# Product-key experts on one core: passes of 32 tokens with all heads instead of 128 tokens with two heads

## The chip, the core and the metric

The kernel runs on one core of a Trainium2 chip. Its engines work side by side: TensorE (PE, with its weight loads PEld), VectorE (DVE), ScalarE (ACT), GpSimd (POOL) and SyncE (SP), and 16 DMA engines move data. The metric is device time in microseconds, and less is better. A time is a median over runs.

## The reference

One step of a decoder layer for 512 new tokens of one sequence and 4 tokens of each of 8 running sequences, so 544 tokens of 1024 channels, all float32. After two recurrent branches comes the part that the change touches, an expert mixer with product keys:

```python
q = (tb @ w_q).reshape(blk, PEER_HEADS, 2, PEER_HALF)            # 8 heads, two halves of 128
s = jnp.einsum('thsk,hsnk->thsn', q, sub_keys)                   # 128 keys per half
sv, si = lax.top_k(s, PEER_TOPK)                                 # the best 16 of each half
cand = sv[:, :, 0, :, None] + sv[:, :, 1, None, :]               # 256 pairs
fv, fi = lax.top_k(cand.reshape(...), PEER_TOPK)                 # the best 16 pairs are the experts
g = jax.nn.softmax(fv, axis=-1)
act = jax.nn.gelu(jnp.einsum('thkd,td->thk', u_emb[idx], tb))
return jnp.einsum('thk,thkd->td', g * act, v_emb[idx])
```

There are 16384 experts, each a row u of 1024 numbers (its dot product with the token gives the activation) and a row v of 1024 numbers (added to the output with weight g times gelu). Each token uses 8 heads times 16 experts. The output is added to the residual and passes a last RMSNorm.

## The kernel before

The program is written engine by engine, and each engine's instructions run in the order of the code. Semaphores join the engines. The tables u and v lie side by side in HBM, so that one row of 8 KB holds both.

**Queries and scores.** 16 units of the weight stream give 16 query blocks (one head and half each) of 128 channels by 544 tokens. TensorE computes a unit (48 matmuls at L404), ScalarE copies it to `qs`, and one unit later TensorE multiplies it with the keys: four products of 128 tokens (L752) and one of the 32 sample tokens (L754). ScalarE copies the scores to `SC`. VectorE picks experts for the first pass while the later units run.

**Expert passes.** There are 17 passes. A pass takes 128 (token, head) partitions by 32 slots. In passes 0 to 15 the partitions are the 128 tokens of a tile, and the 32 slots are two heads of 16 experts; four passes make a tile complete. In pass 16 the 32 sample tokens stand four times on the partitions, each copy with two of the eight heads. Per slot:

- GpSimd gathers 128 rows of 8 KB by indirect DMA (L1331) into one of eight ring buffers. `gathers` waits until the slot that used the buffer before has been read by TensorE (`slot_free`, counted slot by slot).
- VectorE multiplies u with the token's channels and sums (L1768, called a dot below).
- After every two slots (GROUP = 2) five small VectorE instructions and a tanh on ScalarE (L1134) make the weights (L1772 to L1777).
- ScalarE writes each slot's weight on a diagonal 128x128 matrix (L1141), and TensorE multiplies it with v: two products of 128x128 by 512 columns (L788), summed in PSUM over all 32 slots of the pass. Each float32 product shows as two matmul records.

At the end of a pass `flush` (L1786) adds the sum to the residual; TensorE's next pass waits for that. `iteration` first copies the tile's channels to `tb` (L1796). The choice of experts for coming passes (`route_keys`, `route_pairs`, `route_rows`) is cut into pieces and stands between the groups. Passes 1 to 15 are one hardware loop on each of the four engines; passes 0 and 16 are straight code.

After pass 16 a product with `sel` (L799) adds the four copies of the sample tokens, and the last norms and stores follow.

## Time and profile before

| | us |
|---|---|
| time, median of 3 runs (2709.21 to 2720.2) | 2710.64 |
| time of the profiled execution | 2708.6 |
| its span, first to last instruction | 2706.6 |
| expert passes in it, first dot to last flush, 17 passes | 1518.8 |
| mean granted TensorE clock over the span | 0.908 |

All rows quoted below are of that one execution. The page gives shares of the whole span; the expert passes are the last 56% of it and have their own limits, so they are read by stretches. A granted clock of 1.00 is 2.4 GHz and 0.50 is 1.2 GHz.

### The profile page before, as it was taken

To read this page: it belongs to the slowest core of one execution; us is meant where nothing else is said; L and a number is where in the kernel's file an instruction comes from. 1 tells how busy PE (TensorE), PEld (TensorE's weight loads), DVE (VectorE), ACT (ScalarE), POOL (GpSimd) and SP (SyncE) were. 2 spreads that over 40 slices of the span, in tenths; PEclk is the share of its full clock that TensorE was granted. 3 is DMA by queue.
4 is the path that set the end of the run, shared out by engine and by line. 5 is a ranking of instruction groups with operands and counts; after the bars stand their busy time and mean duration, and the time that the engine had idled before them with its cause. 6 is when DMAs were issued, how large, how long until landed. Compare 5 with 4: busy or idle time off the path is not lost.

```text
span 2706.6 us, 34195 instructions
## 1 busy us (share of the span) xinstructions
PE 2130.6 (79%) x9927; PEld 1409.1 (52%) x9927; DVE 1767.8 (65%) x4439; ACT 657.1 (24%) x1597; POOL 1091.2 (40%) x822
## 2 busy tenths in 40 slices
PE   6988899999988898986777677766776676668776
PEld 6987778889977898952222223222322222223222
DVE  5887721143288434158787778777877787778785
ACT  4334300132255224321111111111111111111112
POOL 2553224365433342344444344434443443344342
PEclk9999967799998999999989898989989998898898
DMA  3220023222311232279999999999999999899997
GB/s 140 80 77 1 1 79 139 102 77 86 109 63 47 75 113 71 85 296 391 407 363 362 363 412 360 371 371 396 362 364 372 401 373 359 355 400 360 374 381 287
DMA packets 101508, 664.75 MB, mean 246 GB/s; under 512 B 11744, under 2 KB 12000, under 8 KB 29056
## 3 DMA queue, kind: packets, MB, share of 16 engines
q0 software_dynamic: 78336, 570.46, 52.7%
q1 hardware_dynamic: 20160, 71.92, 7.9%
q10 hardware_dynamic: 2880, 20.97, 2.0%
q8 instruction: 38, 0.62, 0.1%
q14 instruction: 94, 0.77, 0.1%
HBM read 650.38 MB, written 12.14 MB: 245 GB/s over the span
## 4 chain that ended last, share of the span: by engine, by line
DVE 33%; PE 25%; issue 24%; DMA 10%; POOL 4%; ACT 3%; DVEq 1%; POOLq 0%; SPq 0%; ACTq 0%
PE ps L404 12%; DMA s_r<-in_uv,s_gidx 9%; DVE s_r L1768 7%; PE ps L788 5%; DVE s_r L1380 4%; POOL s_r_rounded L1178 3%; DVE s_h L1768 2%; PE ps L641 2%; ACT s_gth L1134 1%; DVE s_r L1712 1%; PE ps L653 1%; DVE s_g L1773 1%; DVE s_g L1776 1%; DVE s_g L1772 1%; DVE s_g L1774 1%
## 5 line engine op out<-in xcount | busy, mean ns | idle before, releaser
L788 PE MATMUL ps<-s_r 128*128 128x512 f32 x1632 | 789.4, 632 | 236.5 <-ACT s_r L1141 235.6
L404 PE MATMUL ps<-s_r_rounded 128*128 128x272 f32 x5760 | 766.9, 296 | 35.7 <-POOL s_r_rounded L1178 10.6
L404 PEld LDWEIGHTS ps<-s_r_rounded 128*128 128x128 f32 x5760 | 753.4, 195 | 46.5 <-issue 28.2
L1331 POOL DMA_INDIRECT s_r<-in_uv,s_gidx x408 | 488.9, 1198 | 531.3 <-PE ps L788 441.5
L788 PEld LDWEIGHTS ps<-s_r 128*128 128x128 f32 x1632 | 309.6, 199 | 709.5 <-ACT s_r L1141 388.0
L1768 DVE CUSTOM_DVE_ANT_0 s_r<-s_r 128x1024 f32<-128x1024 f32 x408 | 486.9, 1222 | 59.6 <-DMA s_r<-in_uv,s_gidx 56.6
L1178 POOL TENSOR_TENSOR s_r_rounded<-s_r,s_r_rounded 128x1024 fp32r<-128x1024 f32 x120 | 305.5, 2547 | 469.6 <-ACT s_r_rounded L815 469.6
L788 PE MATMUL ps<-s_h,s_r 128*128 128x512 f32 x544 | 298.0, 698 | 208.6 <-ACT s_r L1141 208.6
L788 PEld LDWEIGHTS ps<-s_h,s_r 128*128 128x128 f32 x544 | 115.7, 224 | 385.9 <-ACT s_r L1141 252.2
L1134 ACT ACTIVATE s_gth<-s_g 128x2 f32<-128x2 f32 x272 | 55.4, 204 | 1036.8 <-DVE s_g L1774 1036.8
L1331 POOL DMA_INDIRECT s_h<-in_uv,s_gidx x136 | 156.1, 1148 | 344.5 <-PE ps L788 320.5
L815 ACT ACTIVATE s_r_rounded<-s_r 128x1024 fp32r<-128x1024 f32 x120 | 126.5, 1055 | 437.4 <-PE ps L404 437.2
L1141 ACT ACTIVATE s_r<-s_con,s_slot_w 128x128 f32<-128x128 f32 x544 | 188.7, 394 | 135.7 <-DVE s_slot_w L1777 134.2
L1768 DVE CUSTOM_DVE_ANT_0 s_h<-s_h,s_r 128x1024 f32<-128x1024 f32 x136 | 161.5, 1224 | 7.8 <-DVE s_tk_i L1716 5.1
L1380 DVE SCALAR_TENSOR_TENSOR s_r<-s_r,s_par 128x600 f32<-128x600 f32 x96 | 141.3, 1471 | 12.0 <-DVE s_r L1380 0.8
L1543 DVE TENSOR_TENSOR s_h<-ps,s_h 128x2048 f32<-128x2048 f32 x8 | 18.3, 2291 | 134.4 <-PE ps L653 134.4
L1776 DVE SCALAR_TENSOR_TENSOR s_g<-s_gth,s_act_z 128x2 f32<-128x2 f32 x272 | 43.8, 161 | 73.5 <-ACT s_gth L1134 73.5
L1796 DVE COPY s_r<-s_r 128x1024 f32 (+1 forms) x17 | 13.1, 768 | 79.6 <-issue 79.4
L1231 POOL TENSOR_TENSOR s_r<-s_r,s_ed 128x2048 f32<-128x2048 f32 (+1 forms) x5 | 19.3, 3860 | 112.3 <-DVE s_r L1462 83.7
L641 PEld LDWEIGHTS ps<-s_c_s,s_h 128*128 128x128 f32 x256 | 51.3, 311 | 8.8 <-issue 8.8
L1569 DVE TENSOR_TENSOR s_r<-s_r 128x544 f32<-128x544 f32 x16 | 11.9, 744 | 66.4 <-ACT s_r L977 66.4
L1594 DVE SCALAR_TENSOR_TENSOR s_r<-s_r,ps 128x544 f32 x8 | 5.8, 721 | 75.6 <-PE ps L404 75.6
(242 smaller groups left out, 1932.2 us busy)
## 6 DMA issues: line engine op xcount, KB each, us to landing
s_r<-in_wstream SPq DMA_DIRECT2D x120, 512.0 KB, 3.3
s_h<-in_sample_h_in ACTq DMA_DIRECT2D x8, 1024.0 KB, 5.0
out_sample_h_out<-s_h ACTq DMA_DIRECT2D x8, 1024.0 KB, 3.9
s_r<-in_uv,s_gidx POOLq DMA_INDIRECT x408, 10.2
s_r<-in_x SPq DMA_DIRECT2D x4, 544.0 KB, 6.8
s_r<-in_x SPq DMA_DIRECT2D x1, 2176.0 KB, 8.4
s_h<-in_uv,s_gidx POOLq DMA_INDIRECT x136, 9.0
out_y_prompt<-s_r SPq DMA_DIRECT2D x4, 512.0 KB, 9.9
```

The source lines that it names most:

```text
L404: last = pe.matmul(ps[:, 2 * p + h, 0:HALF], fr(wp[:, k, :]), fr(xp[:, k, h * HALF:(h + 1) * HALF]), start=start and k == 0 and t == 0, st ...
L641: last = pe.matmul(inter_out[:, k, b, :], h0[:, j, k * P:(k + 1) * P], c_s[:, k // 4, :].rearrange("p (b l) -> p b l", l=DEC_L)[:, b, :], ...
L653: last = pe.matmul(ps[:, 4 + g, :], bm[0:n, j, g * NST:(g + 1) * NST], xs2[0:n, g * 512:(g + 1) * 512], start=True, stop=True)
L788: last = pe.matmul(ps[:, h, :], diag[:, s % 4, :], ring[s % RING][:, D_MODEL + 512 * h:D_MODEL + 512 * (h + 1)], start=s == 0, stop=s == S ...
L815: act.activation(fr(whi[:, slot % 2]), wring[:, slot], ACT.Copy).then_inc(w_hi, 1)
L1134: act.activation(gth[:], g3[:], ACT.Tanh, scale=GELU_S).then_inc(gl_th, 1)
L1141: act.activation(diag[:, sl % 4, :], ident, ACT.Copy, scale=slot_w[:, j, q * GROUP + s:q * GROUP + s + 1]).then_inc(diag_ready, 1)
L1178: pool.tensor_tensor(fr(wring[:, slot]), wring[:, slot], fr(whi[:, slot % 2]), ALU.subtract).then_inc(w_lo, 1)
L1331: pool.indirect_dma_start(ring[sl % RING], None, a["uv"], bass.IndirectOffsetOnAxis(ap=gidx[:, j, s:s + 1], axis=0)).then_inc(gath[sl % RI ...
L1380: ch.link(dve.scalar_tensor_tensor(out=o, in0=row[:, k:k + CONVN], scalar=pcol(weights, blk, k), in1=o, op0=ALU.mult, op1=ALU.add))
L1768: ch.step(dve.tensor_tensor_reduce(out=u, in0=u, in1=tb, scale=1.0, scalar=0.0, op0=ALU.mult, op1=ALU.add, accum_out=act_z[:, j, k:k + 1]))
L1776: ch.link(dve.scalar_tensor_tensor(out=g1[:], in0=gth[:], scalar=1.0, in1=z, op0=ALU.add, op1=ALU.mult))
```

## The change

Each of the 17 passes now takes 32 tokens with all eight heads. Partition 32q + t is token t with heads 2q and 2q + 1; the 32 slots are again two heads of 16 experts. The number of passes, slots and gathered bytes is the same. What differs:

- The score products write straight in that layout: for each of four key blocks, 17 groups by 4 strips, each 32 tokens by 128 keys. The order of the query weights is permuted on the way in. Scores of four query blocks are computed together and copied with one ScalarE instruction.
- The token rows are put on the partitions four times by four DMAs from SP per pass (`tbg`, two buffers), for every pass. The copy to `tb` on VectorE is gone.
- Gelu and weights are made for four slots at once (BATCH = 4). The weight operand is `sel` (128x32) times the slot weight, one ScalarE instruction for each slot.
- The four products of a batch go to four strips of 32 output partitions, each with its own slot's v: `ps[32c:32c+32]`. Ring buffers come free by the batch (`v_free`). The sums of passes alternate between two pairs of PSUM banks.
- ScalarE copies a pass's four strips out (`empty`), and TensorE adds them with `sel` (`total`) during the next pass. `flush` runs once for every tile of 128 tokens, a pass later, and the last norm of a tile follows it.
- All passes are straight code; there is no loop. Routing for pass g + 1 (both slot halves) stands in pass g.

On TensorE, from the last query units to the first pass, before (L404 query units, L752 and L754 scores, L788 expert values):

```order
L404 MATMUL ps<-s_r_rounded 128x272 x48
L747 REGISTER_ALU
L752 ISA
L752 MATMUL ps<-s_r 128x128 x4
L754 MATMUL ps<-s_r 32x128
L772 REGISTER_ALU
L772 COMPARE_AND_BRANCH
L752 MATMUL ps<-s_r 128x128 x4
L754 MATMUL ps<-s_r 32x128
L788 MATMUL ps<-s_h,s_r 128x512 x4
L788 MATMUL ps<-s_r 128x512 x12
```

The same place now (L415 query units, L766 scores, L805 values):

```order
L415 MATMUL ps<-s_r_rounded 128x272 x192
L766 MATMUL ps<-s_r 32x128 x68
L415 MATMUL ps<-s_r_rounded 128x272 x144
L766 MATMUL ps<-s_r 32x128 x68
L805 MATMUL ps<-s_h,s_r 32x512
L805 MATMUL ps<-s_r 32x512 x3
L805 MATMUL ps<-s_h,s_r 32x512
L805 MATMUL ps<-s_r 32x512 x11
```

Five score products per unit have become 68 for every four units, and the last 68 stand behind the last unit. A batch is eight products of 32 rows instead of eight of 128 for the same four slots.

On VectorE, the turn from one looped pass to the next before (L1768 dots, L1772 to L1777 weights, L1796 the copy to `tb`, L1786 flush, L1721 and L1709 the start of a routing piece):

```order
L1776 SCALAR_TENSOR_TENSOR s_g<-s_gth,s_act_z 128x2
L1777 TENSOR_TENSOR s_slot_w<-s_g,s_gw 128x2
L1839 UNCONDITIONAL_BRANCH
L1839 ISA
L1796 COPY s_r<-s_r 128x1024
L101 ISA
L1784 REGISTER_ALU
L1786 ISA
L1786 TENSOR_TENSOR s_r<-ps,s_r 128x1024
L1721 ISA
L1721 COPY s_r<-s_r 128x256
```

The same turn now (L1754 dots, L1763 to L1771 weights of four slots, L1708 to L1715 the first routing piece):

```order
L1767 SCALAR_TENSOR_TENSOR s_g<-s_gth,s_act_z 128x4
L1771 TENSOR_TENSOR s_slot_w<-s_g,s_gw 128x4
L1754 ISA s_h,s_act_z<-s_h 128x1024
L1754 ISA s_act_z 128x1
L1754 ISA s_r,s_act_z<-s_r,s_h 128x1024
L1754 ISA s_act_z 128x1
L1708 MAX s_tk_v<-s_r 128x8
L1710 MAX_INDEX s_tk_i<-s_tk_v,s_r 128x8
L1711 MATCH_REPLACE s_r<-s_tk_v,s_r 128x128
```

Between the last weights of one pass and the first dot of the next nothing is left.

The core of the diff:

```diff
+GT = 32
+GROUPS = NCH * 4 + 1
 RING = 8
-GROUP = 2
+BATCH = 4
...
+        tbg = h0[:, 0, :].rearrange("p (a b) -> p a b", b=D_MODEL)
+        ring = [h0[:, 1, :]] + [R1[:, i * ROW:(i + 1) * ROW] for i in range(4)] + [R3[:, i * ROW:(i + 1) * ROW] for i in range(3)]
...
+            for g in range(GROUPS):
+                if g >= 2:
+                    sp.wait_ge(dotted, (g - 1) * SLOTS)
+                t0 = GT * (g % 4)
+                for q in range(4):
+                    sp.dma_start(tbg[GT * q:GT * (q + 1), g % 2, :], H2T[t0:t0 + GT, g // 4, :]).then_inc(tb_full[g % 2], 16)
...
+            def scores(i):
+                pe.wait_ge(q_ready, 4 * (i + 1))
+                if i:
+                    pe.wait_ge(sc_ready, i)
+                for g in range(GROUPS):
+                    for q in range(4):
+                        hs = (2 * q + i // 2) * 2 + i % 2
...
+                        last = pe.matmul(out, qs[:, q, GT * g:GT * (g + 1)], keys[:, hs, :], start=True, stop=True)
...
+            def total(g):
+                pe.wait_ge(evac_done, g + 1)
...
+                    last = pe.matmul(ps[o:o + GT, 2 + h, :], cc("sel"), evac[:, h, :], start=True, stop=True)
...
+            def values(g):
+                bank = 4 * (g % 2)
...
+                for b in range(BATCHES):
+                    if g and b == 4:
+                        total(g - 1)
+                    pe.wait_ge(lhs_ready, (g * BATCHES + b + 1) * BATCH)
                     for h in range(2):
-                        last = pe.matmul(ps[:, h, :], diag[:, s % 4, :],
-                                         ring[s % RING][:, D_MODEL + 512 * h:D_MODEL + 512 * (h + 1)],
-                                         start=s == 0, stop=s == SLOTS - 1)
-                    last.then_inc(slot_free, 1)
+                        for c in range(BATCH):
+                            n = g * SLOTS + b * BATCH + c
+                            last = pe.matmul(ps[GT * c:GT * (c + 1), bank + h, :], lhs[:, b % 2, c, :],
+                                             ring[n % RING][:, D_MODEL + 512 * h:D_MODEL + 512 * (h + 1)],
+                                             start=b == 0, stop=b == BATCHES - 1)
+                    last.then_inc(v_free, 1)
...
+            def batch(g, b):
+                m = g * BATCHES + b
+                act.wait_ge(gl_in, m + 1)
+                act.activation(gth[:, 0:BATCH], g3[:, 0:BATCH], ACT.Tanh, scale=GELU_S).then_inc(gl_th, 1)
...
+                for c in range(BATCH):
+                    k = b * BATCH + c
+                    act.activation(lhs[:, b % 2, c, :], cc("sel"), ACT.Copy,
+                                   scale=slot_w[:, k:k + 1]).then_inc(lhs_ready, 1)
...
+            def gather(g, s):
+                n = g * SLOTS + s
+                if s % TOPK == 0:
+                    pool.wait_ge(idx_ready, 2 * g + s // TOPK + 1)
+                if n == 1:
+                    pool.wait_ge(unit_done, UNITS)
+                if n >= RING:
+                    pool.wait_ge(v_free, (n - RING) // BATCH + 1)
...
             dve.wait_ge(sc_ready, 2)
-            route(0, 0, 0)
+            route(0, 0)
             dve.wait_ge(sc_ready, 4)
-            route(0, 1, 1)
+            route(0, 1)
+            dve.wait_ge(sc_ready, 5)
+            for g in range(GROUPS):
+                dve.wait_ge(tb_full[g % 2], 64 * (g // 2 + 1))
+                for s in range(SLOTS):
+                    if g + 1 < GROUPS:
+                        for j in range(2):
+                            if s == 11 * j + 2:
+                                route_keys(g + 1, j, 0)
+                            if s == 11 * j + 5:
+                                route_keys(g + 1, j, 1)
+                            if s == 11 * j + 8:
+                                route_pairs()
+                            if s == 11 * j + 11:
+                                route_rows(g + 1, j)
+                    if g and g % 4 == 0 and s == 25:
+                        flush(g // 4 - 1)
+                    if g and g % 4 == 0 and s == 30:
+                        final_norm(g // 4 - 1)
+                    dot(g, s)
+                    if s % BATCH == BATCH - 1:
+                        slot_weights(g, s // BATCH)
```

`scores(i)` counts as done when ScalarE has copied it (`sc_ready`); the fourth copy comes after the last unit.

## Rows read from the trace of the kernel before

**Rows 1.** The page: DMA share in 40 slices and GpSimd's queue (q0): packets, MB, share.

```profile
DMA  3220023222311232279999999999999999899997
q0 software_dynamic: 78336, 570.46, 52.7%
```

**Rows 2.** Busy us by engine and stretch, clock, DMA share, GB/s.

```profile
1176.70:2695.50 1518.80, 1076.08 (x2176) 425.30 (x2176) 1188.82 (x3702) 264.28 (x891) 639.04 (x539) 0.90 0.94 376
1195.00:1219.00 24.00, 18.14 (x40) 7.18 (x40) 16.72 (x50) 4.28 (x14) 10.64 (x10) 1.00 1.01 421
1978.00:1984.00 6.00, 0.06 (x1) 0.06 (x1) 5.00 (x21) 0.71 (x3) 0.00 (x0) 0.53 1.02 422
1984.00:1989.00 5.00, 5.00 (x7) 2.16 (x8) 4.35 (x17) 0.48 (x3) 0.50 (x1) 0.54 0.32 133
```

**Rows 3.** Waits of the expert passes: us in total, times, longest.

```profile
POOL s_r L1331 <- PE ps L788: 441.5, 216, 14.6
DVE s_r L1796 <- issue: 79.4, 14, 6.0
```

**Rows 4.** Timeline of one pair of slots: start, us, engine, line, operation, idle before.

```profile
1202.77 1.23 DVE L1768 CUSTOM_DVE_ANT_0 s_r<-s_r 128x1024 f32<-128x1024 f32 x1 [1.25 <-DMA s_r<-in_uv,s_gidx]
1205.06 0.16 DVE L1777 TENSOR_TENSOR s_slot_w<-s_g,s_gw 128x2 f32<-128x2 f32 x1
1205.25 0.69 ACT L1141 ACTIVATE s_r<-s_con,s_slot_w 128x128 f32<-128x128 f32 x2 [0.42 <-DVE s_slot_w L1777]
1205.71 3.70 PE L788 MATMUL ps<-s_r 128*128 128x512 f32 x8 [1.28 <-ACT s_r L1141]
1208.47 1.31 POOL L1331 DMA_INDIRECT s_r<-in_uv,s_gidx  x1 [2.32 <-PE ps L788]
```

**Rows 5.** Gathers issued at 1901.47 and at 1904.90: count, us from issue to landing.

```profile
s_h<-in_uv,s_gidx POOLq DMA_INDIRECT x1, 5.5
s_r<-in_uv,s_gidx POOLq DMA_INDIRECT x1, 8.3
```

**Rows 6.** TensorE timeline: strips of 64 rows, full products, and weight loads at low clock.

```profile
213.10 1.09 PE L465 MATMUL ps<-s_con,s_DA 128*64 128x128 f32 x16
214.13 1.16 PE L532 MATMUL ps<-s_r 128*128 128x128 f32 x8
1985.81 0.33 PEld L788 LDWEIGHTS ps<-s_h,s_r 128*128 128x128 f32 x1 [0.52 <-issue]
1986.67 0.33 PEld L788 LDWEIGHTS ps<-s_h,s_r 128*128 128x128 f32 x1 [0.52 <-issue]
```

**Rows 7.** Groups of the page: xcount, busy and mean ns, idle before and its cause.

```profile
L1134 ACT ACTIVATE s_gth<-s_g 128x2 f32<-128x2 f32 x272 | 55.4, 204 | 1036.8 <-DVE s_g L1774 1036.8
```

**Rows 8.** VectorE timeline at a loop turn and, from 2598.40, at the turn in straight code.

```profile
1969.24 0.16 DVE L1777 TENSOR_TENSOR s_slot_w<-s_g,s_gw 128x2 f32<-128x2 f32 x1
1975.12 0.77 DVE L1796 COPY s_r<-s_r 128x1024 f32 x1 [5.73 <-issue]
...
2598.40 0.69 DVE L1796 COPY s_r<-s_r 128x1024 f32<-128x1024 f32 x1
2602.75 1.22 DVE L1786 TENSOR_TENSOR s_r<-ps,s_r 128x1024 f32<-128x1024 f32 x1 [3.66 <-PE ps L788]
```

**Rows 9.** Timeline of routing on VectorE: second key piece, pairs, and the end of the rows.

```profile
1080.77 0.29 DVE L1709 MAX8 s_tk_v<-s_r 128x8 f32<-128x128 f32 x1
1082.68 0.18 DVE L1726 CAST s_tk_if<-s_tk_i 128x32 f32<-128x32 uint32 x1
1088.67 0.17 DVE L1744 SCALAR_TENSOR_TENSOR s_gidx<-s_tk_sel 128x16 uint32<-128x16 f32 x1
```

**Rows 10.** Timeline of a query unit and its scores, and of the first dot.

```profile
1083.55 6.27 PE L404 MATMUL ps<-s_r_rounded 128*128 128x272 f32 x48
1089.66 1.05 PE L752 MATMUL ps<-s_r 128*128 x8
1176.69 1.23 DVE L1768 CUSTOM_DVE_ANT_0 s_h<-s_h,s_r 128x1024 f32<-128x1024 f32 x1
```

More of the change, by code:

```diff
@@ L743, in _ @@
             pe.wait_ge(ld_late, 32)
-            def scores(q, p, first=False):
-                pe.wait_ge(q_ready, q + 1)
-                if not first:
-                    pe.wait_ge(sc_ready, q - 1)
-                for i in range(NCH):
-                    pe.matmul(ps[:, 4 + p, i * CH:(i + 1) * CH], qs[:, p, i * CH:(i + 1) * CH], keys[:, q, :],
-                              start=True, stop=True)
-                pe.matmul(ps[0:DEC, 6 + p, 0:NKEYS], qs[:, p, SEQ:TOK], keys[:, q, :],
-                          start=True, stop=True).then_inc(sc_mm, 1)
@@ L757, in query @@
-            def query(i, j, first=False):
-                if not first:
-                    pe.wait_ge(q_ready, i * RINGW + (j - 1))
-                unit(i * RINGW + (U_WQ + j), j, j % 2, hn_parts, blocks=(hn_ready, KT) if first and j == 0 else None)
+            def scores(i):
[5 more added lines that the diff above has]
+                        hs = (2 * q + i // 2) * 2 + i % 2
+                        out = ps[GT * q:GT * (q + 1), 4 + g // 4, (g % 4) * NKEYS:(g % 4 + 1) * NKEYS] if g < GROUPS - 1 \
+                            else ps[GT * q:GT * (q + 1), i, 512 - NKEYS:512]
+                        last = pe.matmul(out, qs[:, q, GT * g:GT * (g + 1)], keys[:, hs, :], start=True, stop=True)
+                last.then_inc(sc_mm, 1)
@@ L793, in _ @@
-            experts(0)
-            with pe.Fori(1, ITERS) as it:
-                experts(it)
-            pe.wait_ge(flushed, ITERS)
-            for h in range(2):
-                last = pe.matmul(ps[0:DEC, 2 + h, :], cc("sel"), X2T[:, TILES - 1, 512 * h:512 * (h + 1)],
-                                 start=True, stop=True)
-            last.then_inc(fin_mm, 1)
+            for i in range(HS // RINGW):
+                for j in range(RINGW):
+                    n = i * RINGW + j
+                    if n >= 2:
+                        pe.wait_ge(q_ready, n - 1)
+                    unit(U_WQ + n, j, j % 2, hn_parts, blocks=(hn_ready, KT) if n == 0 else None)
+                    if i and j == 0:
+                        scores(i - 1)
@@ L1158, in _ @@
-            squares = SC[:, 0:2, :].rearrange("p a b -> p (a b)")
-            softmax_exp(1)
-            experts(0)
-            with act.Fori(1, ITERS - 1) as it:
-                experts(it)
-            experts(ITERS - 1, True)
-            act.wait_ge(flushed, ITERS + 1)
-            token_norms(NCH, TILES, TILES, squares)
+            for n in range(HS):
+                keep_query(n)
+                if n >= RINGW and n % RINGW == 1:
+                    keep_scores(n // RINGW - 1)
+                if n == 2 * RINGW + 3:
+                    softmax_exp(0)
@@ new lines, in _ @@
+            softmax_exp(1)
+            for g in range(GROUPS):
+                for b in range(BATCHES):
+                    if b == 2 and g + 1 < GROUPS:
+                        softmax_exp(2 * g + 2)
+                    if b == 3 and g:
+                        empty(g - 1)
+                    if b == 4 and g + 1 < GROUPS:
+                        softmax_exp(2 * g + 3)
+                    if b == 6 and g and g % 4 == 0:
+                        token_norm(g // 4 - 1)
+                    batch(g, b)
@@ L1747, in route_rows @@
+                dve.wait_ge(ex_ready, 2 * g + j + 1)
                 ch.link(dve.reciprocal(tk_r[:], tk_sum[:]))
[L1748 to L1778 removed]
@@ L1851, in _blocks @@
+            flush(NCH)
+            final_norm(NCH)
 def _blocks(w, kb):
```

334 lines of the change are left out of this document (124 added, 210 removed).

## The prediction

> **What bounds the kernel now.** I read the page first, then the expert passes by stretches, then the waits of GpSimd and VectorE, then one pair of slots in the timeline. The page shows that the DMA engines are nine tenths busy through the expert passes, and that GpSimd's queue, the gathers, carries 570 of the 665 MB moved [rows 1]. The passes take 1518.8 us, that is 89.3 for each of 17. In them the DMA share is 0.94 at 376 GB/s, while in the steady stretch it is 1.01 at 421 GB/s [rows 2]. A slot is 128 rows of 8 KB, 1,048,576 bytes; at 421 GB/s that is 2.49 us, so 32 slots need 79.7 us and 17 passes 1355. The DMA bounds the passes, and 164 us are lost beside it. They are lost at the turns: the stretch after one shows the DMA at 0.32 of its share [rows 2]. There GpSimd waits for TensorE to free a ring buffer, 14.6 us at the longest [rows 3], because VectorE stands still in front of L1796 for 5.7 us at each loop turn (79.4 us in 14 of them) [rows 3, 8], then flushes and routes before its first dot.
>
> So two questions decide: what becomes of the turns, and whether a ring of eight buffers that comes free four at a time still keeps the DMA supplied.
>
> **What goes.** The loop turn (5.7 us), the copy to `tb` (0.8) and 15 of the 17 flushes (1.2 each) leave VectorE, and 16 rounds of small weight instructions per pass become 8. A round takes 1.22 us from the dot's end to the weights' end [rows 4], so 9.8 us per pass go. Of the turn not all can be had: in straight code the stall is gone, but VectorE waits 3.66 us for TensorE's last product [rows 8]. The new code avoids that too, since the flush comes a pass later. VectorE's pass is then 32 dots at 1.15 (36.8), 8 rounds (9.8) and two routings of some 10.5 (below), 68 us. It no longer bounds anything; nor does TensorE. Were the ring long enough, a pass would be 79.7 plus the token rows (four DMAs of 128 KB, 0.5 MB at 421 GB/s, 1.25), that is 80.9 us: 142 us less in all. This is the most the change can bring to the passes.
>
> At the loop turn the Trainium skill bears on this (Runtime: NRT & Kernel Launch, Instruction fetch mechanics): a taken branch out of the instructions already fetched stops the engine until its target has come, so it advises to unroll. The trace agrees with 5.73 us.
>
> **What the batch adds.** The four buffers of batch b come free together and are gathered into for batch b + 2. The loop of one batch, from the landing of its fourth gather, by [rows 4] where nothing else is named:
>
> - dot 1.23, then the round 1.22, then 0.03 to ScalarE;
> - four weight operands of 128x32. The trace has 0.20 for 128x2 [rows 7] and 0.345 for 128x128 (half of 0.69). Bounds 0.8 and 1.4 for four; I take 0.24 each, 0.96, nearer the small one. Then 0.11 to TensorE, which waits for all four;
> - eight products, 16 records. Does it run four strips at once? Sixteen records of 64-row strips, alternating between two strips, take 1.09 us, where eight full records of as many columns take 1.16 [rows 6]: two strips run side by side. Four strips don't occur in the trace. Bounds: four at a time 4 record times, two at a time 8; I take 4, since the two strips show no loss at all. A record time is 0.86 us at a granted clock of 0.54 [rows 2, 6], half of that at full clock, where eight records take 3.70 [rows 4], so 0.3 stays as the tail of the last. TensorE would work under 4 us in every 10 and idle the rest. Idle from the last pass's end, it stood at 0.53 and came back at 0.54 [rows 2]. So I take the low clock: 4 x 0.86 + 0.3 = 3.7 (full clock 2.0);
> - from the products' end to the gather 0.76: the first slot's four records end at 1205.71 + 1.7 + 0.3 = 1207.71, and the gather starts at 1208.47;
> - issue to landing 5.5 where nothing is ahead [rows 5], and three more slots at 2.49, 7.47.
>
> Sum 21.0 us for a loop, in which two batches pass: 10.5 us per batch, 83.9 per pass. Supply alone would give 10.1. The ring is the bound, by little, and every microsecond in the loop counts half, eight times a pass.
>
> Two things lengthen it. Routing stands in front of single dots: the second key piece takes 1.9 us, pairs and rows together 6.2 [rows 9], and some 0.5 for the softmax scale; say 1.9, 1.9, 3.3 and 3.4. Where dots wait for landings, each leaves 2.49 - 1.15 = 1.3 us. Pieces before slots 11 and 19 (the last of a batch) delay it by 2.1 and 2.0, that before slot 22 by 0.8 at slot 23; the others fit. 4.9 us in one of two alternating chains are 2.5 per pass. And gathers into an emptied queue come slowly: issued at 1901.47 and landed 5.5 later, at 1906.97; the one issued at 1904.90 landed at 1913.2 [rows 5], with one more between. Two slots in 6.2 us instead of 5.0: 1.2 late per burst. Bounds 0 (the queue rarely empties) and 4.8 per pass (each burst pays); I take 4.0, since the ring-bound case empties it every time. Below 0 it can't be, as the DMA share is full already.
>
> A pass: 83.9 + 2.5 + 4.0 = 90.4 us, 1536.8 for 17, against 1518.8: **+18.0**. Bounds from these pieces alone (operands 0.8 to 1.4, restarts 0 to 4.8): 85.8 to 93, or -60 to +62.
>
> The rule that speaks against the change is in the Trainium skill (TensorE: Matmul & The Clock Gate, Why this matters for your kernels): idle gaps between bursts of matmuls bring the slow clock back. The trace agrees, with 0.53 after the turn. Of the strips the same page (Part 3: Packing small matmuls) says that outputs in different groups of 32 partitions run at the same time, and gives 2.38 times the speed for three; by that the batch takes somewhat more than my 4 record times, and the sum would move by some us per pass to the slow side. No row here shows three or four.
>
> **Start and end.** The first dot came at 1176.69 [rows 10], 5.1 us after the last unit. Now the last scores, their copy and the whole second routing stand behind that unit. 68 products are 136 records: at 0.068 per record with two strips [rows 6] 9.2 us, with four 4.6; I take 5. The copy of 2048 columns: between 128x2 and 128x128 an element costs 1.1 ns, 2.3 us. Query copy 0.6. Routing 1.9 + 8.1 + 0.5 = 10.5 [rows 9]. First dot 18.4 after the unit: +13.3. The eight buffers are full by then, and nothing can be gathered until the first batch is through, so the delay stays. The scores before the last unit: 15 times 1.3 us (1.05 and the sample's 0.3) [rows 10] against three times 5: -4.5. At the end, a batch instead of a pair before the last product, and a copy by ScalarE (its 128x1024 some 1.1): +3. Final norms of earlier tiles and the stores lie beside other work. SP's copies of token rows wait for dots of a pass before and are done long ahead; if not, the first dot of a pass would wait some 3 us.
>
> Sum: 2708.6 (the profiled execution) + 18.0 + 13.3 - 4.5 + 3 = 2738.4. The median of before is 2 us above the profiled execution, which I leave out. A measurement of this kernel can tell 0.5% (13.5 us) from no change.
>
> **Rivals.**
>
> 1. *The loop is short enough.* Full clock (2.0 us instead of 3.7), or operands at 0.2 and no slow restarts, make the supply the bound: 80.9 plus what routing still delays, some 2.5 to 4.5: 83.4 to 85.4 a pass. Taken 84.9: 17 x -4.4 = -75, with +12 for start and end 2646. For it: the DMA never starves in the steady stretch, where one slot at a time is freed [rows 2]. Against: the clock at 0.53.
> 2. *Strips run two at a time, or one after another.* 8 record times, partly at the higher clock as the burst is long: 5.6 to 7.2 us. Loop 22.9 to 24.5, per pass 92 to 98, plus 6.5: 98.5 to 104.5. +156 to +258, and +16: 2880 to 2980. That is the case in which the change doesn't do what it says. For it: every float32 product has two records for the same strip, which can't run together. Against: two strips show twice the rate.
> 3. *Straight code stalls.* VectorE's code grows to 17 passes. If each block of new code cost a stop like the 5.7 of a turn, ten of them would come on top: 2738 + 57 = 2795. Against: pass 16, straight behind the loop, starts without a stop [rows 8].
>
> **Chances.** Forecast 0.53, rival 1 0.25, rival 2 0.13, rival 3 0.09. The forecast's own range is 2690 to 2790. The range for the time takes rival 1 in and stops before most of rival 2: 2645 to 2860. Slower by over 0.5%: 0.66 of the forecast (35), rivals 2 and 3 (22): 0.57. Faster: nearly all of rival 1 and a tenth of the forecast: 0.29. Within: 0.14.
>
> **What would show it.** The turn: no idle of 5.7 on VectorE, and no wait for the flush. The loop: GpSimd's gathers in bursts of four, each burst 0.8 after the batch's last product, DMA share below 0.95 throughout instead of 1.01 with dips. TensorE: four records starting together, batches of 3.7 us, granted clock near 0.5. A pass of 90 us between first dots; the first dot 18 us after the last unit. I am wrong if the DMA share stays at 1.0 between batches (then rival 1), if a batch takes over 5 us on TensorE (rival 2), or if VectorE waits for "issue" inside passes (rival 3).

## The result: 2846 us, slower by 5%, and the profile after

| | before | after |
|---|---|---|
| median, us | 2709.9 (2709.1 to 2720.2, 4 runs) | 2846.3 (2845.0 to 2851.5, 4 runs) |
| ratio, with its 95% interval | | 1.050 (1.047 to 1.053) |
| profiled execution: span | 2706.6 | 2842.7 |
| first dot, last dot | 1176.69, 2688.82 | 1181.73, 2822.87 |
| a pass (mean of 12, first dot of pass 3 to first dot of pass 15, counted from 0) | 89.9 | 97.5 |

The direction was forecast (+30 us), the size was not (+136). The two spans split it: the first dot is 5.0 us later, first to last dot takes 1641.1 us instead of 1512.1 (+129.0), the end 2.0 more. So nearly all of it is in the passes. All means by pass or by batch below are over the same 12 passes, worked out from the start times of the dots and gathers in the timeline and from the landings. Batches 0 to 7 of a pass are its groups of four slots.

The page after: TensorE's granted clock, DMA share and queues, and VectorE's dots. Through the passes the DMA share of [rows 1] was mostly 9, and now about every third slice is an 8. Queue q1, which carries the copies of token rows, had a share of 7.9% and has 8.8%.

```profile
PEclk9999967999998999756556655666665556566555
DMA  3220033222211322589988998899989898998997
q0 software_dynamic: 78336, 570.46, 51.5%
q1 hardware_dynamic: 23040, 80.05, 8.8%
L1754 DVE CUSTOM_DVE_ANT_0 s_r<-s_r,s_h 128x1024 f32<-128x1024 f32 x476 | 580.0, 1224 | 406.6 <-DMA s_r<-in_uv,s_gidx 404.3
```

The passes by stretches, after (columns as in [rows 2]: stretch, length, busy us of five engines, clock, DMA share, GB/s): the whole, then an emptied queue and the time that follows it.

```profile
1300.00:2800.00 1500.00, 473.27 (x2044) 83.73 (x2036) 966.12 (x2701) 181.50 (x706) 529.08 (x494) 0.60 0.91 352
...
2022.00:2024.50 2.50, 1.31 (x8) 0.00 (x0) 2.36 (x8) 0.00 (x0) 0.38 (x1) 0.50 0.43 174
2024.50:2026.00 1.50, 0.00 (x0) 0.00 (x0) 0.98 (x2) 0.00 (x0) 1.20 (x2) 0.50 0.46 76
2026.00:2030.00 4.00, 0.00 (x0) 0.00 (x0) 2.47 (x8) 0.94 (x5) 2.17 (x3) 0.50 0.89 326
```

The dips of the loop turns are gone, but the share is 0.91 at 352 GB/s where [rows 2] has 0.94 at 376. The dips that took their place come four times a pass, one in front of each even burst: in the pass from 2046 to 2143 the share falls to 0.49, 0.35, 0.35 and 0.00 in stretches of 2 us. Behind one, a share of 0.89 moves only 326 GB/s, where the steady stretch of before moved 421 at 1.01. GpSimd waits for TensorE in front of each burst and no longer in front of single gathers, to answer [rows 3] (us in total, times, longest):

```profile
POOL s_h L1335 <- PE ps L805: 634.0, 67, 21.2
...
POOL s_r L1335 <- PE ps L805: 301.4, 67, 7.2
```

134 waits are one for each batch after the first two. Those in front of `s_h`, which holds slot 0 of the eight, belong to batches with an even number and are twice as long. "Even" and "odd" below are the numbers of batches; a burst is the four gathers that a freed batch lets start. One batch from its last dot to the next gather, in answer to [rows 4]:

```profile
2001.73 1.23 DVE L1754 CUSTOM_DVE_ANT_0 s_r<-s_r,s_h 128x1024 f32<-128x1024 f32 x1 [1.21 <-DMA s_r<-in_uv,s_gidx]
2004.03 0.16 DVE L1771 TENSOR_TENSOR s_slot_w<-s_g,s_gw 128x4 f32<-128x4 f32 x1
2004.29 0.96 ACT L1155 ACTIVATE s_r<-s_con,s_slot_w 128x32 f32<-128x32 f32 x4 [0.49 <-DVE s_slot_w L1771]
2005.30 3.51 PE L805 MATMUL ps<-s_r 128*32 128x512 f32 x16 [6.46 <-ACT s_r L1155]
2009.63 1.63 POOL L1335 DMA_INDIRECT s_r<-in_uv,s_gidx  x1 [4.58 <-PE ps L805]
```

From the dot's end (2002.96) to the gather are 6.67 us; my terms were 1.22 + 0.03 + 0.96 + 0.11 + 3.7 + 0.76 = 6.78. This half of the loop was right to 0.1 us. The other half was not. These are two even bursts: the gathers of the first (slots 24 to 27) start at 2024.12 and no routing stands in front of its dots; the second (slots 0 to 3 of the next pass) starts at 2046.69. Columns: start, us, engine, line, operation, idle before and what ended it.

```profile
2024.12 0.93 POOL L1335 DMA_INDIRECT s_h<-in_uv,s_gidx  x1 [9.12 <-PE ps L805]
2029.58 1.23 DVE L1754 CUSTOM_DVE_ANT_0 s_h<-s_h 128x1024 f32<-128x1024 f32 x1 [0.41 <-DMA s_h<-in_uv,s_gidx]
2033.78 1.23 DVE L1754 CUSTOM_DVE_ANT_0 s_r<-s_r,s_h 128x1024 f32<-128x1024 f32 x1 [1.83 <-DMA s_r<-in_uv,s_gidx]
2036.24 1.22 DVE L1754 CUSTOM_DVE_ANT_0 s_r<-s_r,s_h 128x1024 f32<-128x1024 f32 x1 [1.23 <-DMA s_r<-in_uv,s_gidx]
2038.69 1.22 DVE L1754 CUSTOM_DVE_ANT_0 s_r<-s_r,s_h 128x1024 f32<-128x1024 f32 x1 [1.22 <-DMA s_r<-in_uv,s_gidx]
...
2046.69 1.58 POOL L1335 DMA_INDIRECT s_h<-in_uv,s_gidx  x1 [7.15 <-PE ps L805]
2053.57 1.23 DVE L1754 CUSTOM_DVE_ANT_0 s_h<-s_h 128x1024 f32<-128x1024 f32 x1 [1.26 <-DMA s_h<-in_uv,s_gidx]
2057.39 1.22 DVE L1754 CUSTOM_DVE_ANT_0 s_r<-s_r,s_h 128x1024 f32<-128x1024 f32 x1 [2.59 <-DMA s_r<-in_uv,s_gidx]
2062.57 1.23 DVE L1754 CUSTOM_DVE_ANT_0 s_r<-s_r,s_h 128x1024 f32<-128x1024 f32 x1 [2.16 <-DMA s_r<-in_uv,s_gidx]
2066.09 1.23 DVE L1754 CUSTOM_DVE_ANT_0 s_r<-s_r,s_h 128x1024 f32<-128x1024 f32 x1 [2.29 <-DMA s_r<-in_uv,s_gidx]
...
2074.18 1.36 POOL L1335 DMA_INDIRECT s_h<-in_uv,s_gidx  x1 [11.03 <-PE ps L805]
```

My sum had the fourth slot landed 13.0 us after its burst's first gather (5.5 + 3 x 2.49). Here it is 14.6 in the first burst, where only the second slot is late (4.2 instead of 2.5 after the first), and 19.4 in the second, into which SyncE puts the four copies of token rows:

```profile
2051.10 2.90 SPq L395 DMA_DIRECT2D s_h<-s_r  x4
```

In the mean the loop of an even batch takes, from its first gather to the next one into the same buffer:

| batches | 0 to 2 | 2 to 4 | 4 to 6 | 6 to 0 | sum |
|---|---|---|---|---|---|
| forecast, bare | 21.0 | 21.0 | 21.0 | 21.0 | 84 (90.5 with its 6.5 for routing and restarts) |
| after | 26.7 | 24.1 | 24.2 | 22.4 | 97.4 |

Last, start and end, to answer [rows 10]: scores, their copy, and the last total.

```profile
1165.44 3.92 PE L766 MATMUL ps<-s_r 128*32 128x128 f32 x136 [0.71 <-ACT s_r L1110]
...
1169.43 1.88 ACT L1114 ACTIVATE s_r<-ps 128x2048 f32<-128x2048 f32 x1 [4.04 <-PE ps L766]
...
2831.23 3.55 PE L790 MATMUL ps<-s_r,s_con 128*32 128x512 f32 x4 [1.14 <-ACT s_r L1137]
```

### The profile page after: what moved, and what is told of

Same layout as the page of the kernel before. It is cut to its first block, busy times and chain, and to the rows that moved or that the text cites. A ratio compares the mean times of both kernels' runs of the same rounds, so it can differ in the third digit from the quotient of the medians.

```text
span 2842.7 us, 30578 instructions
## 1 busy us (share of the span) xinstructions
PE 1567.5 (55%) x10375; PEld 1072.1 (38%) x10375; DVE 1636.6 (58%) x3698; ACT 590.4 (21%) x1412; POOL 1030.9 (36%) x822
## 4 chain that ended last, share of the span: by engine, by line
issue 27%; DMA 25%; PE 23%; DVE 12%; POOL 9%; ACT 2%; DVEq 0%; POOLq 0%; SPq 0%; ACTq 0%
DMA s_r<-in_uv,s_gidx 24%; PE ps L415 12%; POOL s_r L1335 5%; PE ps L805 5%; DVE s_r L1381 3%; POOL s_r_rounded L1184 3%; DVE s_r L1754 2%; PE ps L652 2%; ACT s_r L1155 1%; PE ps L664 1%; POOL s_h L1335 1%; PE ps L506 1%; PE ps L766 1%; DVE s_r L1379 1%; DMA s_rgh<-in_rgh 1%
## 5 line engine op out<-in xcount | busy, mean ns | idle before, releaser
L1754 DVE CUSTOM_DVE_ANT_0 s_r<-s_r,s_h 128x1024 f32<-128x1024 f32 x476 | 580.0, 1224 | 406.6 <-DMA s_r<-in_uv,s_gidx 404.3
L415 PE MATMUL ps<-s_r_rounded 128*128 128x272 f32 x5760 | 764.0, 295 | 37.0 <-POOL s_r_rounded L1184 11.8
L415 PEld LDWEIGHTS ps<-s_r_rounded 128*128 128x128 f32 x5760 | 752.6, 195 | 45.9 <-issue 26.3
L805 PE MATMUL ps<-s_r 128*32 128x512 f32 x1904 | 484.8, 1043 | 418.2 <-ACT s_r L1155 418.2
L805 PE MATMUL ps<-s_h,s_r 128*32 128x512 f32 x272 | 240.6, 1040 | 724.7 <-ACT s_r L1155 724.7
L805 PEld LDWEIGHTS ps<-s_h,s_r 128*32 128x32 f32 x272 | 36.5, 159 | 913.4 <-ACT s_r L1155 591.1
L1335 POOL DMA_INDIRECT s_h<-in_uv,s_gidx x68 | 91.0, 1338 | 634.2 <-PE ps L805 634.0
L805 PEld LDWEIGHTS ps<-s_r 128*32 128x32 f32 x1904 | 79.4, 158 | 619.9 <-ACT s_r L1155 530.6
L1149 ACT ACTIVATE s_gth<-s_g 128x4 f32<-128x4 f32 x136 | 27.9, 205 | 1145.7 <-DVE s_g L1765 1145.7
L1155 ACT ACTIVATE s_r<-s_con,s_slot_w 128x32 f32<-128x32 f32 x544 | 130.1, 310 | 66.9 <-DVE s_slot_w L1771 66.9
L1754 DVE CUSTOM_DVE_ANT_0 s_h<-s_h 128x1024 f32<-128x1024 f32 x68 | 83.2, 1223 | 77.6 <-DMA s_h<-in_uv,s_gidx 77.1
L1708 DVE MAX8 s_tk_v<-s_r 128x8 f32<-128x128 f32 x68 | 19.6, 288 | 82.2 <-ACT s_r L1114 82.0
L652 PE MATMUL ps<-s_c_s,s_h 128*128 128x4 f32 x256 | 52.1, 340 | 1.1 <-ACT s_r L963 1.1
L1570 DVE TENSOR_TENSOR s_r<-s_r 128x544 f32<-128x544 f32 x16 | 11.9, 743 | 66.3 <-ACT s_r L989 66.3
```

Of the source, the lines that this page charges most:

```text
L415: last = pe.matmul(ps[:, 2 * p + h, 0:HALF], fr(wp[:, k, :]), fr(xp[:, k, h * HALF:(h + 1) * HALF]), start=start and k == 0 and t == 0, st ...
L652: last = pe.matmul(inter_out[:, k, b, :], h0[:, j, k * P:(k + 1) * P], c_s[:, k // 4, :].rearrange("p (b l) -> p b l", l=DEC_L)[:, b, :], ...
L805: last = pe.matmul(ps[GT * c:GT * (c + 1), bank + h, :], lhs[:, b % 2, c, :], ring[n % RING][:, D_MODEL + 512 * h:D_MODEL + 512 * (h + 1)] ...
L1155: act.activation(lhs[:, b % 2, c, :], cc("sel"), ACT.Copy, scale=slot_w[:, k:k + 1]).then_inc(lhs_ready, 1)
L1335: pool.indirect_dma_start(ring[n % RING], None, a["uv"], bass.IndirectOffsetOnAxis(ap=gidx[:, g % 2, s:s + 1], axis=0)).then_inc(gath[n % ...
L1754: dve.tensor_tensor_reduce(out=u, in0=u, in1=tbg[:, g % 2, :], scale=1.0, scalar=0.0, op0=ALU.mult, op1=ALU.add, accum_out=act_z[:, s:s + ...
```

## The experiments

All times are medians; the ratio is to the kernel before, measured beside each, with its interval. "A pass" is the mean defined above, of one profiled execution.

One thing beside the passes moves these times by some 10 us. The last 136 score records take 3.9 us in `after` and in eight other traces, and 12.7 to 14.3 us in those of `ring10`, `rows_once`, `routes_first`, `rows_once_routes`, `rowspe8` and `ring10_rowspe_routes`, where TensorE stops between them ("issue", 4 to 6 us in all) and its granted clock is 0.74 to 0.81 instead of 1.0. The first dot is late by as much. Why was not tested. So small differences are read from the column "a pass".

| run | us | ratio | a pass |
|---|---|---|---|
| after | 2846.3 | 1.050 (1.047 to 1.053) | 97.5 |
| ring10 | 2638.8 | 0.972 (0.968 to 0.976) | 84.9 |
| rows_once | 2806.2 | 1.034 (1.029 to 1.038) | 94.8 |
| routes_first | 2820.7 | 1.039 (1.034 to 1.044) | 95.7 |
| before_free4 | 2916.8 | 1.074 (1.069 to 1.080) | 101.8 |
| dose | 2929.9 | 1.079 (1.077 to 1.081) | 102.5 |
| warm | 2855.7 | 1.052 (1.050 to 1.054) | 98.2 |
| batch2 | 2664.0 | 0.981 (0.979 to 0.983) | 87.2 |
| batch2_ring10 | 2639.8 | 0.973 (0.971 to 0.974) | 85.6 |
| warm_even | 2832.9 | 1.043 (1.041 to 1.046) | 97.0 |
| half | 2732.2 | 1.007 (1.005 to 1.009) | 91.1 |
| ring9 | 2714.6 | 1.001 (0.999 to 1.003) | 89.2 |
| ring10_rowspe | 2578.0 | 0.950 (0.949 to 0.952) | 81.4 |
| rows_once_routes | 2777.0 | 1.024 (1.020 to 1.028) | 92.5 |
| rowspe8 | 2809.7 | 1.036 (1.034 to 1.039) | 94.8 |
| ring10_rowspe_routes | 2586.1 | 0.954 (0.952 to 0.957) | 81.6 |

### Is it the loop from landing to free buffers?

The loop theory: eight buffers, freed four at a time, don't cover landing, dots, weights and products, and what stands in that loop sets the pace. The rival: the DMA's own work (slower gathers, token rows) sets it.

**ring10**, two more buffers:

```diff
-RING = 8
+RING = 10
+            + [R2[:, XB * TOK + 2 * D_MODEL:XB * TOK + 2 * D_MODEL + ROW], R4[:, WORK - 4 * TOK:WORK - 4 * TOK + ROW]]
...
+                if n == RING - 1:
+                    pool.wait_ge(sc_mm, HS // RINGW)
```

> The changed kernel with ten ring buffers instead of eight (the two more lie where the query copies and old convolution channels were). If the loop of the buffers bounds it (theory: ten buffers make the loop of 10 slots, so a pass falls from 97.3 us towards the DMA's 81), the time falls by 8 to 14 us a pass, 140 to 230 in all, to 2620 to 2710. If it is the DMA that has become slower (the copies of token rows, 4 KB pieces between the gathers), more buffers change little: over 2800.

2638.8 us. Two buffers take 208 us away, though batch, strips, rounds and clock are the same. Its passes, columns as above:

```profile
1300.00:2590.00 1290.00, 470.38 (x2016) 83.55 (x2016) 950.71 (x2677) 180.05 (x700) 564.62 (x489) 0.62 1.01 404
```

The DMA share is 1.01 over the whole stretch; TensorE's clock, 0.62, is as low as in the slow kernel. So once the queue stays full, neither clock nor strips nor straight code cost anything that shows.

**ring9**, one more buffer:

```diff
-RING = 8
+RING = 9
+            + [R2[:, XB * TOK + 2 * D_MODEL:XB * TOK + 2 * D_MODEL + ROW]]
```

> The changed kernel with nine buffers: one gather of each burst is issued a batch earlier, so 2.5 us of transfer stand in the queue when the others are freed. Loop theory: the empty stretch between two bursts (1.1 us per batch by the DMA packets) and most of the slow first packets go; a pass of 85 to 89 us, 2640 to 2710, between eight buffers (97.5 us a pass) and ten (84.9). If slow restarts depend on the bursts and not on the emptied queue, it stays above 2750.

2714.6 us, a pass of 89.2, 5 us above the expected range and the same time as the kernel before. One buffer is worth 8.3 us a pass, the second 4.3, after which the supply is the bound.

**dose**, one unused full product in front of every batch:

```diff
+                    for _ in range(1):
+                        pe.matmul(ps[:, 6, :], ident, H2T[:, 0, 0:512], start=True, stop=True)
```

> The changed kernel with one more full product (512 columns, its result unused) on TensorE in front of every batch's products: some 1.7 us at the low clock, put into the loop from landing to free buffers. Loop theory (the eight buffers come free four at a time, and what stands in the loop counts half per batch): 1.7 x 4 loops x 17 passes = +116 us, 2940 to 2970. Supply theory (the DMA engines, with slow restarts and token rows, set the pace, and TensorE is beside the path): within 15 us of 2846. If the clock rises from the work that is added, the loop theory gives less, 2850 to 2900.

2929.9 us, +83.6, 10 us under the expected 2940. From last dot to gather it takes 1.6 us more (8.3), and a pass 5.0 more, where the loop theory says 4 x 1.6 = 6.4. The rest is given back while the landings wait.

**half**, 8 of 16 records per batch:

```diff
-                    for h in range(2):
+                    for h in range(1):
```

> The changed kernel without the products of the second 512 value columns (their part of the output is not computed): 8 records per batch instead of 16, 1.7 us less between the weights and the free buffers of every batch, nothing else. Loop theory: minus 6.8 us a pass at most, by the same slope as one product more gave (5.0 us a pass for 1.6 us): 2846 - 85 to - 116, 2730 to 2760. Supply theory: within 15 us of 2846.

2732.2 us, -114, as expected: the tail, from the end of a batch's last dot to the gather it sets free, is 5.09 instead of 6.72, and a pass 6.4 shorter (4 x 1.63 = 6.5). A microsecond in the loop counts four times a pass, as the prediction had it.

**before_free4**, the kernel before with its buffers freed in fours:

```diff
-                        pool.wait_ge(slot_free, it * SLOTS + (sl - RING + 1))
+                        pool.wait_ge(slot_free, it * SLOTS + ((sl - RING) // 4 * 4 + 4))
```

> The kernel before with one part of the change alone: GpSimd waits until the four slots of a batch have all been read before it gathers into the first of them; weights stay in pairs and products per slot. Loop theory: the last of four slots is read some 7 us after the first, so the supply starves oftener; +30 to +100 us, 2740 to 2810. Rival (freeing by four costs nothing, the loss lies in what precedes the products): within 15 us of 2710.

2916.8 us: +201, more than twice what I expected, and slower than the changed kernel. Coarse freeing alone costs the kernel before 11.9 us a pass, without any strips. It has the turns besides, and four of its slots occupy TensorE for two pairs of 3.7 us one after the other.

**batch2**, two slots per batch, two batches side by side in the four strips:

```diff
-BATCH = 4
+BATCH = 2
...
-                            last = pe.matmul(ps[GT * c:GT * (c + 1), bank + h, :], lhs[:, b % 2, c, :],
+                            d = 2 * (b % 2) + c
+                            last = pe.matmul(ps[GT * d:GT * (d + 1), bank + h, :], lhs[:, b % 2, c, :],
...
-                                             start=b == 0, stop=b == BATCHES - 1)
+                                             start=b < 2, stop=b >= BATCHES - 2)
```

> The changed kernel with batches of two slots instead of four: two batches share the four strips, buffers come free two at a time, and VectorE has 16 rounds of small instructions per pass as before the change. Loop theory: the loop of a batch is 5.5 + 2.5 + 1.2 + 6.3 = 15.5 us for eight buffers, under the 19.9 that the supply needs, so the DMA never empties: VectorE's work (80 us a pass) and the supply (81) bound it together, 83 to 87 a pass, 2610 to 2690. If instead the work in straight code, the token rows by SP or the products in strips cost the time, it stays above 2800.

2664.0 us with eight buffers. The same work, freed in twos, is 182 us faster and beats the kernel before by 1.9%: it is the batch of four that empties the queue. Here the DMA share is full:

```profile
1300.00:2620.00 1320.00, 713.21 (x2016) 123.46 (x2016) 1038.99 (x3281) 218.18 (x821) 538.64 (x488) 0.74 1.00 394
```

**batch2_ring10**, both:

> Batches of two slots and ten buffers. Loop theory: the loop is no limit with either, so nothing is added: within 15 us of the better of the two alone (2639 with ten buffers). With ten buffers and batches of four a pass takes 84.9 us of which 82.7 are the gathers' own packets; here VectorE has 9.8 us more of small instructions, and if that is what bounds it, it is slower than 2639 by 10 to 60 us.

2639.8, the same as ten buffers alone, but the start hides a difference: first to last dot takes 1438.2 us against 1427.2 in `ring10`, 0.7 us a pass more (85.6 against 84.9), and `ring10` has the late first dot. VectorE's eight additional rounds cost little, not nothing.

### Which of the two chains, and the clock

**warm**, six unused products behind every batch:

```diff
                     last.then_inc(v_free, 1)
+                    for _ in range(6):
+                        pe.matmul(ps[:, 6, :], ident, H2T[:, 0, 0:512], start=True, stop=True)
```

> The changed kernel with six full products (results unused) on TensorE behind every batch, after its buffers are set free, so that TensorE is not idle between batches. Loop theory: with the full clock the products of a batch take 2.0 instead of 3.7 us, the loop 22.7 instead of 24.4, a pass 90.7: 2730 (2715 to 2760). If the clock stays low, six products take 10 us, stand in front of the next batch at times and make it slower than 2846. Supply theory: 2846 whatever the clock.

2855.7, nothing gained, a miss. TensorE in the timeline of this run (L805 the products, L810 the unused ones):

```profile
2003.91 1.06 PE L805 MATMUL ps<-s_h,s_r 128*32 128x512 f32 x1 [6.98 <-ACT s_r L1157]
2004.77 1.06 PE L805 MATMUL ps<-s_h,s_r 128*32 128x512 f32 x1
2005.62 1.06 PE L805 MATMUL ps<-s_h,s_r 128*32 128x512 f32 x1
2006.48 1.06 PE L805 MATMUL ps<-s_h,s_r 128*32 128x512 f32 x1
2007.49 6.31 PE L810 MATMUL ps<-s_r,s_con 128*128 128x512 f32 x12
...
2013.73 1.92 PE L805 MATMUL ps<-s_r 128*32 128x512 f32 x16
2015.59 5.42 PE L810 MATMUL ps<-s_r,s_con 128*128 128x512 f32 x12
```

An even batch comes after 7 us of idle and runs at 1.2 GHz (a record every 0.86 us), the odd one right behind it at 2.4 GHz (16 records in 1.92). Odd tails fell to 5.6 us on average, even ones stayed at 6.75, and the loop at 24.6: the odd burst's first dot came 10.8 instead of 9.3 us after its gather, for it stands in the queue behind the even one. What the odd chain wins, it waits. That is against the prediction's "counts half": a gain in one of the two chains alone brought nothing.

**warm_even**, 12 behind odd and 3 behind even batches:

```diff
+                    for _ in range(12 if b % 2 else 3):
```

> The changed kernel with 12 unused full products behind every batch with an odd number and 3 behind every even one. With six behind each, the trace showed that only the odd batches ran at the full clock (5.1 to 5.7 us from the last dot to the next gather, the even ones 6.7 to 6.8 as before), and that the time did not move. Theory: the even batches are the ones whose gathers go into an empty queue; their loop alone sets the pace, and the odd ones wait behind them in the queue. Then the even loop 1.7 us shorter gives up to 6.8 us a pass, less where the odd chain takes over: 2750 to 2800. If both chains count alike, as my prediction had it, the six products would have brought 30 us already, and this brings about as much as that, nothing: 2840 to 2860. If twelve products last longer than the gap, the time is above 2860.

2832.9, 13 us less: below the 2840 to 2860 of equal chains, not the 2750 to 2800 either. Twelve products last 10.6 us and stand in front of the even batch at times, so its tail fell only to 6.44. That is inconclusive for the even chain alone; `half`, which shortens both, is the clean test.

### What lengthens the landings

**rows_once** leaves out 60 of the 68 copies of token rows (the output of passes 2 to 16 isn't computed from their own rows):

```diff
+                if g >= 2 and g % 4 != 2:
+                    continue
...
-                for q in range(4):
+                for q in range(4 if g < 2 else 0):
...
-                dve.wait_ge(tb_full[g % 2], 64 * (g // 2 + 1))
+                dve.wait_ge(tb_full[g % 2], 64)
```

> The changed kernel with the token rows copied for the first two passes only; later passes use those rows again, so 60 of the 68 copies of 128 KB are left out and the output is not the reference's. If the copies slow the gathers beyond their own 1.25 us a pass, the time falls by the missing 7 us a pass or more, below 2740. If the loop bounds it, at most their own share goes: 2820 to 2846.

2806.2, -40: below the 2820 of the one theory and far above the 2740 of the other. The loop from batch 0 to 2 fell from 26.7 to 23.2, that from 2 to 4 took 1.0 of it back.

**routes_first**, each routing piece in front of a batch's first dot:

```diff
-                            if s == 11 * j + 2:
+                            if s == 16 * j:
...
-                            if s == 11 * j + 5:
+                            if s == 16 * j + 4:
```

(and `+ 8`, `+ 12`; the second exponential moves from batch 4 to 6)

> The changed kernel with each piece of routing in front of the first dot of a batch (slots 0, 4, 8, 12, 16, 20, 24, 28) instead of slots 2, 5, 8, 11, 13, 16, 19, 22. By the loop theory a piece in front of the last dot of a batch lengthens the loop: my sum had 2.5 us a pass for it, 42 in all: 2800. If pieces anywhere make VectorE late by their sum, the time stays within 15 us of 2846.

2820.7, -26 and short of the expected 2800; some 10 us are lost to the late first dot. The loops 2 to 4 and 4 to 6 fall from 24.1 and 24.2 to 22.6 and 23.1; the loop 0 to 2 rises from 26.7 to 27.2.

**rows_once_routes**, both edits together:

> The changed kernel with both edits that were run alone: the token rows are copied only for the first two passes (output of the others is not computed from their own rows), and the routing pieces stand one in front of each batch's first dot. Alone they gave 40 and 26 us. If what is left over of the error is the slow restarts of the DMA queue, the two add up: 2780 (2770 to 2790), a pass of 93 to 94 us, still 3 to 4 above the 90.4 of my sum. If the two were the whole error, a pass comes to 90.4 or less, below 2735.

2777.0, as expected: a pass of 92.5, with even loops of 23.7, 22.7, 23.3 and 22.7 us, nearly alike. With rows and routing out of the way each still takes 1.7 to 2.7 more than 21.0. All of it is in the landings: the fourth gather lands 15.1 us after its burst's first one starts, even or odd, where my sum has 13.0, and the last dot starts 0.02 us behind that landing.

**rowspe8** spreads the token rows on TensorE into banks 6 and 7, from where ScalarE copies them to `tbg`; the four DMAs are dropped:

```diff
+            def token_rows(g):
+                n = P if g < GROUPS - 1 else DEC
+                if g:
+                    pe.wait_ge(tb_full[(g - 1) % 2], (g - 1) // 2 + 1)
+                for h in range(2):
+                    for q in range(4):
+                        last = pe.matmul(ps[GT * q:GT * (q + 1), 6 + h, :], ident[0:n, GT * (g % 4):GT * (g % 4 + 1)],
+                                         H2T[0:n, g // 4, 512 * h:512 * (h + 1)], start=True, stop=True)
+                last.then_inc(rep_mm, 1)
...
+            def rows_out(g):
+                act.wait_ge(rep_mm, g + 1)
+                if g >= 2:
+                    act.wait_ge(dotted, (g - 1) * SLOTS)
+                act.activation(tbg[:, g % 2, :], ps[:, 6:8, :], ACT.Copy).then_inc(tb_full[g % 2], 1)
```

> The changed kernel with eight buffers as it is, and the token rows spread by TensorE and ScalarE instead of four DMAs per pass (full output). With ten buffers this gave 61 us (3.5 per pass). Here the loop sets the pace: leaving the copies out gave 2.4 per pass, and the eight products (3.5 us at the low clock) stand once per pass in front of a batch, which gives back up to 1.7: 2800 to 2835. If the DMA's bytes counted in full as with ten buffers, 2785.

2809.7, the same as leaving the copies out. The added products cost nothing that shows.

**ring10_rowspe**, the same with ten buffers:

> Ten buffers, and the token rows are spread over the four strips by eight products with parts of the identity on TensorE and one copy by ScalarE, in place of four DMAs of 128 KB per pass. With ten buffers the DMA engines are full (packets of 85.3 us in a pass of 84.9), 2.3 us of it the token rows: supply theory gives 82.6 us a pass, 2600 (2590 to 2615). If the added products (3.5 us at the low clock, once a pass in front of a batch) or the copy stand in the path, it is at or above 2639.

2578.0 us, below the 2590 to 2615 expected, and 5.0% (4.8 to 5.1) faster than before: the fastest version. Its passes:

```profile
1300.00:2530.00 1230.00, 496.50 (x2228) 91.69 (x2232) 940.03 (x2644) 191.61 (x708) 562.97 (x486) 0.64 1.00 415
```

A DMA share of 1.00 moves 415 GB/s now, 404 with the copies. Half a megabyte of them costs a full queue 3.5 us a pass (84.9 to 81.4). Of the 61 us between the two runs some 10 are `ring10`'s late first dot.

**ring10_rowspe_routes**:

> The fastest version so far (ten buffers, token rows by TensorE, 81.4 us a pass with the DMA engines full) with the routing pieces in front of the batches' first dots. With full DMA engines nothing on VectorE is on the path, so 2578 within 6 us, and only a piece before the first dot of a pass could cost something. If routing still delays the freeing of buffers, it is 10 to 25 us faster.

2586.1, 8 us slower, and all of that is the start: the first dot is 8.9 us later, and first to last dot takes 1374.1 us against 1375.4. Where the queue never empties, the place of the routing wins nothing.

## Why the direction was right and the size wrong

The measured 2846 lies in the stated 2645 to 2860, but above the forecast's own 2690 to 2790; the range had been widened for rival 1 and a part of rival 2, and neither came true.

- **The turn, the flush, the copy.** Right: no idle of 5.7 us is left on VectorE. The DMA dips of the turns are gone.
- **Strips.** Right: four records start together, the next four 0.86 us later, and 16 take 3.2 to 3.64 us, four record times. The scores show it too, 136 records of 128 columns in 3.92 us where I had 4.6 for four at a time and took 5. Rival 2 is out. The Trainium skill (TensorE: Matmul & The Clock Gate, Part 3: Packing small matmuls) gives 2.38 times the speed for three; here four strips take the time of one.
- **Low clock.** Right: granted 0.50 to 0.59 during each of the 136 batches, with 4 to 14 us of idle between them. The Trainium skill (TensorE: Matmul & The Clock Gate, Why this matters for your kernels) says that idle gaps between bursts bring the slow clock back, and the trace of `warm` agrees: the batch behind 7 us of idle is at 1.2 GHz.
- **From last dot to gather.** Right: 6.72 us measured, 6.78 forecast. That a microsecond of it in every batch counts four times a pass is shown by `half` and, less sharply, by `dose`.
- **"Issue to landing 5.5 us where nothing is ahead, and three more slots at 2.49"**, with 2.5 for routing and 4.0 for restarts on top. This is the step that failed. Measured against 21.0, the even loops are longer by 5.7, 3.1, 3.2 and 1.4 us, 13.4 a pass, where I had 6.5. The landings and dots of the even batches split it:
  - Restarts. Where neither routing nor copies stand in the way (batch 6) the fourth gather lands 14.5 us after the burst's start instead of 13.0, and in batches 2 and 4 14.4 and 14.3: some 1.4 for a restart, 5.6 a pass instead of 4.0.
  - Routing. In batches 2 and 4 the last dot also starts 1.85 and 1.98 us behind its landing, since a piece of routing stands before slots 11 and 19. I had those delays right (2.1 and 2.0) and then halved them, as lying in one of two chains; they lie in the even chain, whose loops are longer by them in full: 3.8 instead of 2.5. (`routes_first`, which takes them out alone, gets 1.8 a pass back.)
  - Token rows. In batch 0 the fourth gather lands after 18.6, and `rows_once` takes 3.5 off that loop: the copies of token rows, which I had put at nothing. I had them in the sum of a supply-bound pass (1.25) and left them out of the ring-bound one, because no dot waits for them. They stand in the same DMA engines as the burst on which everything waits.
  - That makes 12.9 of the 13.4; the rest is in batch 0's landings and was not divided further.
- These parts don't add up exactly when they are taken away: routing and rows together give 5.0 a pass of their 7.3, and 8.4 is then left above 84. By the landings and dots of `rows_once_routes` it is all late landings, 2.1 us in each of the four loops, none of it routing. Whether slow restarts alone make them late is open: when an even burst starts there, the odd one's last gather is still 3 us from landing. My upper bound for restarts (4.8) was too low in either reading, as it came from two slots of one burst.
- **Rival 1** named the cure: that the DMA keeps its share where the loop is short enough. Ten buffers show it, 84.9 a pass; my floor of 80.9 was low, by the token rows (3.5, not 1.25) and the gathers' own pace (81.4 / 32 = 2.54 instead of 2.49 us).
- **Rival 3** is out: from the first dot to the last VectorE waits for "issue" 0.6 us in all.
- **Start and end.** First dot +5.0 where I had +8.8 (scores 3.9 and copy 1.9 us instead of 5 and 2.3, and the last unit ended 6.9 us earlier instead of 4.5). That was in part luck: in six of the kernels above the same scores took 12.7 us and more. The end was +2.0 where I had +3.

The sum, with what was measured in place of what was forecast: 129.0 + 5.0 + 2.0 = 136.

## What to carry to other kernels

A ring's worth is not its number of buffers but how many stay full while the oldest is being worked on: before buffers are freed in larger batches, add up one batch's loop (issue, landings, work, release), and compare it with the time that the supply needs to fill the ring. Here the sum was 21.0 us against 19.9, it became 24.4, and a microsecond left out of every batch's loop counted four times a pass; nine buffers were not quite enough, ten were. Two more buffers, or batches of two, turn the same change from 5% slower to 2 to 3% faster. Traffic that no one waits for still costs its time, and more, if it falls into the burst that everyone waits for.

## What was not expected of the hardware

- Four strips of 32 output partitions run float32 products with no loss that shows: 16 records in 3.64 us at the low clock, four times the 0.86 between starts plus a tail.
- A queue that has run empty is slow to start: around the first gather of the burst at 2024.12 it moves 76 GB/s for 1.5 us and then 326 for 4 us, at shares of 0.46 and 0.89, against 421 at 1.01 in the steady stretch before. In even bursts without copies the second gather lands 3.3 to 3.5 us behind the first, in odd ones 2.5.
- Copies of 0.5 MB from SBUF to SBUF cost full DMA engines 3.5 us, 2.8 times what their bytes take at 421 GB/s.
- A mean clock says little of a batch's clock: in `warm` 5.4 us of products and then 7 us of idle left the next batch at 1.2 GHz, while a batch right behind such products ran at 2.4, with a mean granted clock of 0.84 over the passes.
- The same 136 score records took 3.9 us in nine traces and 12.7 to 14.3 in six, with stops on TensorE whose cause is open.
